# First mixer: the mix of a unit's two probabilities on GpSimd in two passes, in place of one pass on VectorE

## What is computed

```python
def diff_attend(q, k, v, lam):
    s = jnp.einsum('bqhcd,bkhcd->bhcqk', q, k, preferred_element_type=jnp.float32) * ATTN_SCALE
    p = jax.nn.softmax(s, axis=-1)
    a = p[:, :, 0] - lam * p[:, :, 1]
    return jnp.einsum('bhqk,bkhe->bqhe', a.astype(v.dtype), v)
```

## Time and profile before

| | us |
|---|---|
| Median of 3 runs | 1674.27 (1674.07 to 1675.11) |
| Profiled execution | 1675.91 |
| Its span | 1674.6 |
| TensorE busy in the span | 1648.6 (98%) |
| VectorE busy | 1127.3 (67%) |
| ScalarE busy | 825.3 (49%) |
| GpSimd busy | 240.7 (14%) |

### The profile page before, as it was taken

How to read it: one execution, slowest core, us unless ns; L and a number is a source line. 1 busy time by engine, 2 the same in 40 slices (tenths; PEclk the granted TensorE clock), 3 DMA queues, 4 the chain that set the end, 5 groups by cost and what they waited for, 6 DMA issues and landing times.

```text
span 1674.6 us, 20880 instructions
## 1 busy us (share of the span) xinstructions
PE 1648.6 (98%) x7900; PEld 1333.8 (80%) x7900; DVE 1127.3 (67%) x1320; ACT 825.3 (49%) x1022; POOL 240.7 (14%) x380
## 2 busy tenths in 40 slices
PE   6999999999999999999999999999999999999999
PEld 3776788887778888788888888888888888888887
DVE  2898778897876764766558756664666567766663
ACT  3426654435475443644446654453544447564442
POOL 0001000000002230123203002240042203002240
PEclk9999999999999999999999999999999999999999
DMA  9686188897448876677655428766676654338660
GB/s 349 221 297 220 51 303 280 312 358 256 162 126 266 265 253 201 178 225 230 213 165 168 126 76 246 219 227 183 201 214 221 213 176 151 101 124 234 210 230 26
DMA packets 250307, 346.50 MB, mean 207 GB/s; under 512 B 16160, under 2 KB 197124, under 8 KB 250208
## 3 DMA queue, kind: packets, MB, share of 16 engines
q1 hardware_dynamic: 236016, 321.95, 58.7%
q0 software_dynamic: 11488, 17.39, 4.3%
q10 hardware_dynamic: 2704, 5.82, 1.0%
HBM read 329.64 MB, written 1.05 MB: 197 GB/s over the span
## 4 chain that ended last, share of the span: by engine, by line
PE 90%; DVE 6%; ACT 2%; issue 1%; DMA 1%; SPq 0%; DVEq 0%
PE bank L467 19%; PE bank L469 19%; PE bank L468 19%; PE bank L837 7%; PE bank L838 7%; PE bank L842 7%; DVE lo L1985 1%; PE bank L1364 1%; PE bank L817 1%; PE bank L1365 1%; PE bank L1367 1%; PE bank L1175 1%; PE bank L493 1%; DMA raw<-in_ada_w 1%; PE bank L1038 1%
## 5 line engine op out<-in xcount | busy, mean ns | idle before, releaser
L1985 DVE TENSOR_TENSOR lo<-raw,hi 128x2048 fp32r<-128x2048 f32 x246 | 563.9, 2295 | 294.2 <-ACT hi L1420 290.8
L1420 ACT ACTIVATE hi<-raw 128x2048 fp32r<-128x2048 f32 x258 | 492.7, 1914 | 315.8 <-PE bank L469 172.1
L467 PE MATMUL bank<-hi,XTh 128*128 128x512 f32 (+1 forms) x1424 | 560.0, 393 | 4.8 <-DVE XTl L2096 4.5
L469 PE MATMUL bank<-hi,XTl 128*128 128x512 f32 (+1 forms) x1424 | 552.5, 388 | 0.0
L468 PE MATMUL bank<-lo,XTh 128*128 128x512 f32 (+1 forms) x1424 | 552.1, 388 | 0.0
L467 PEld LDWEIGHTS bank<-hi,XTh 128*128 128x128 f32 x1424 | 268.0, 188 | 68.5 <-issue 14.9
L469 PEld LDWEIGHTS bank<-hi,XTl 128*128 128x128 f32 x1424 | 268.0, 188 | 55.3
L468 PEld LDWEIGHTS bank<-lo,XTh 128*128 128x128 f32 x1424 | 268.3, 188 | 53.7 <-issue 1.0
L2972 POOL DMA_DIRECT2D HTR<-BLK x320 | 192.4, 609 | 735.6 <-DVE BLK L2482 688.5
L837 PE MATMUL bank<-hi,HTh 128*128 128x512 f32 x528 | 206.4, 391 | 0.0
L838 PE MATMUL bank<-lo,HTh 128*128 128x512 f32 x528 | 205.6, 389 | 0.0
(11 more groups left out here) (391 smaller groups left out, 1453.2 us busy)
## 6 DMA issues: line engine op xcount, KB each, us to landing
raw<-in_ffn_w_in SPq DMA_DIRECT2D x176, 512.0 KB, 4.9
raw<-in_ffn_w SPq DMA_DIRECT2D x132, 512.0 KB, 4.9
raw<-in_ada_w SPq DMA_DIRECT2D x96, 512.0 KB, 5.2
raw<-in_ffn_w_out SPq DMA_DIRECT2D x88, 512.0 KB, 4.1
raw<-in_w_mix_in SPq DMA_DIRECT2D x52, 512.0 KB, 4.7
raw<-in_od_pw_w SPq DMA_DIRECT2D x24, 512.0 KB, 5.5
HTR<-BLK POOLq DMA_DIRECT2D x240, 48.0 KB, 4.2
raw<-in_ev_w_in SPq DMA_DIRECT2D x20, 512.0 KB, 8.5
```

The lines of the kernel that those rows point to most:

```text
L467: pe.matmul(dst, xh, wh, start=start, stop=False)
L469: return pe.matmul(dst, xl, wh, start=False, stop=stop)
L1420: act.activation(hi[r][:, :], raw[g % RAW][:, :], ACT.Copy).then_inc(*up("hi", d))
L1985: dve.tensor_tensor(lo[r][:, :], raw[g % RAW][:, :], hi[r][:, :].bitcast(F32), ALU.subtract).then_inc(*up("lo", d))
```

## The change

The pass L2300 leaves VectorE. GpSimd gets a loop over the twelve units between its DMAs of the Fourier weights and its wait for `o_full`. For each unit it waits for the factor (`diff_rel`), multiplies P1[j] by it in place, waits for itself (`diff_scaled`), and adds P1[j] to P0[j]. The add raises `diff_mixed`, for which TensorE's transposes wait as before. VectorE's reciprocal of unit u waits for `diff_scaled` of u - 2 instead of its own `diff_rel`. The two events move to a semaphore that GpSimd raises.

```diff
--- before.py
+++ after.py
@@ -54,7 +54,7 @@
     "lambdas": "lam_prod lam_sum lam_a lam subg",
     "row_scales": "rstd_in rstd rstd2",
     "diff_scales": "diff_rstd diff_normed",
-    "diff_statistics": "diff_max diff_inv diff_rel diff_mixed",
+    "diff_statistics": "diff_max diff_inv diff_rel",
     "rotated": "rope_part roped",
     "bounds": "lb lb_diff lb_max",
     "ln_rows": "ln_sum ln_mean ln_normed ln_rstd",
@@ -68,7 +68,7 @@
     "modulations": "mods modc ada_part gate_full",
     "down_parts": "down_bias down_gated",
 
-    "hg_decays": "hg_dec hg_tail",
+    "hg_decays": "hg_dec hg_tail diff_scaled diff_mixed",
 
     "row_squares": "sq sq2 sq_in std std2",
     "exponents": "lam_exp lb_exp fox_zrow",
@@ -2289,16 +2289,13 @@
                 st = ST[:, 8 * j:8 * j + 8]
                 dve.wait_ge(*at("diff_exp", (u, 1)))
                 if u >= 2:
-                    dve.wait_ge(*at("diff_rel", u - 2))
+                    dve.wait_ge(*at("diff_scaled", u - 2))
                 dve.reciprocal(INV2[:, 2 * (u % 4):2 * (u % 4) + 2], st[:, 4:6]).then_inc(*up("diff_inv", u))
                 if u >= 2:
                     diff_values(u - 2)
                 dve.wait_ge(*at("diff_inv", u))
                 dve.tensor_scalar(st[:, 2:3], INV2[:, 2 * (u % 4) + 1:2 * (u % 4) + 2], st[:, 4:5], LAM[:, 4:5], ALU.mult,
                                   ALU.mult).then_inc(*up("diff_rel", u))
-                dve.wait_ge(*at("diff_rel", u))
-                dve.scalar_tensor_tensor(out=P0[j][:, :], in0=P1[j][:, :], scalar=st[:, 2:3], in1=P0[j][:, :], op0=ALU.mult,
-                                         op1=ALU.add).then_inc(*up("diff_mixed", u))
 
             def diff_values(u):
                 h, t = units[u]
@@ -2950,6 +2947,13 @@
             for g in range(4):
                 o = (g % 2) * HD
                 pool.dma_start(WB[o:o + HD, g // 2, o:o + HD], A["ev_fourier_w"][0, g, :, :]).then_inc(*up("four_w", g, 16))
+            for u in range(HEADS1 * T):
+                j = u % 2
+                pool.wait_ge(*at("diff_rel", u))
+                pool.tensor_scalar(P1[j][:, :], P1[j][:, :], ST[:, 8 * j + 2:8 * j + 3], None,
+                                   ALU.mult).then_inc(*up("diff_scaled", u))
+                pool.wait_ge(*at("diff_scaled", u))
+                pool.tensor_tensor(P0[j][:, :], P0[j][:, :], P1[j][:, :], ALU.add).then_inc(*up("diff_mixed", u))
             pool.wait_ge(*at("o_full", 3))
             for q in range(4):
                 pool.dma_start(TAPW[32 * q:32 * q + TAPS, :],
```

## The result

| | us |
|---|---|
| Kernel before, median of 4 runs | 1674.34 (1674.07 to 1675.11) |
| Changed kernel, median of 4 runs | 1706.45 (1704.96 to 1706.91) |
| Ratio | 1.0187 [1.0174, 1.0199] |
| Profiled execution after; its span | 1705.99; 1704.7 |

The change costs 32.1 us. The forecast was 21.1, with 1705 as the upper end: the sign was right and the size too small by a third.

A forecast was written before the change was run, and what follows sets the result against it. The prediction took a loop over VectorE and TensorE in the first mixer's stage as the bound, which GpSimd's passes lengthen. Terms 6.9 + 5.0 + 7.7 + 1.5 = 21.1 us gave 1695.4 us, range 1687 to 1705.

The forecast's parts named there:

- The loop: First mixer's stage: next mix waits for TensorE's round; 2.22 us besides the mix, turn 4.26 instead of 2.97.
- VectorE's saving: First mixer's stage: VectorE loses twelve mixes of 0.75 us, which would not count because the loop through GpSimd is longer.
- The late DMAs of the convolution's constants: DMAs at 161.08 before move behind unit 11, near 197 us; the convolution comes much later, so cost nothing.
- I take 0.8, the middle, as it reads one input: GpSimd's multiplication in each unit: 0.8 us, between a memset's 0.549 and a two-input pass's 1.036.
- the add's own term: GpSimd's add of 128x512 f32 in each unit: 1.04 us, from a tensor_tensor row of 1036 ns.
- the exclusion: Units 3 to 5: GpSimd's multiplication waits out VectorE's half split, turns of 5.3 against 3.63; 5.0 us, 3.4 less without it.
- the start: Unit 0's mixed tile comes at 148.0 us, so the work on which unit 2 hangs starts 6.9 us late.
- I take the 6.0 of w_out: Load ahead of GpSimd's first multiplication: 6.0 us, between 1.28 and 8.5.
- That cover takes the longer loop whole, 0: Turn from unit 7 to 8, 4.29 us before with VectorE waiting 1.43 for scores: the longer loop adds 0.
- The clock, 1.5 taken: Pieces behind TensorE's wait of about 8 us for unit 0 run at the lower clock: 1.5 us, ends 0 and 4.
- so this kind of work held the clock before: Argument against rival (b): transposes took 0.66 us at 140 us as at 172 in the kernel before.
- Rival (b): Clock stays low through the whole stage, up to 1.3 us a turn over nine turns: +31 to +33, 1706 us; chance 0.08.

The follow-up runs named there:

- the probe: Changed kernel plus twelve GpSimd passes of 128x512 f32 at its start, three of each form; constant 1494 ns, column 1565, two tiles 1387, broadcast column 1150; total not read.
- the fill: Changed kernel with eight discarded identity matmuls on TensorE ahead of each wait for a mixed tile from unit 2 on; 1701.18 us, ratio 1.016.
- the same edit of the start: Changed kernel with the clearing of WB and its four DMAs behind unit 1; 1706.94 us alone, 1699.55 us with eight identity matmuls ahead of each wait.

## Why the prediction was wrong in size

**The loop was right.** "Everything but the mix is 2.97 - 0.75 = 2.22 us" holds for four lengths of the mix. At full clock GpSimd's part, or VectorE's, gives:

| kernel | the mix, us | turn, us | turn - mix |
|---|---|---|---|
| before | 0.75 | 2.97 | 2.22 |
| add alone on GpSimd | 1.8 | 4.04 | 2.2 |
| broadcast multiplication | 2.42 | 4.63 | 2.2 |
| as changed | 3.0 | 5.18 | 2.2 |

VectorE's saving brought nothing, as the prediction said, and nothing behind the stage gave time back. The late DMAs of the convolution's constants (207.01) did no harm.

**"I take 0.8, the middle, as it reads one input": the term that failed first.** The multiplication took 1.56 us, above even the upper bound of 1.036, and the add 1.26 against 1.04. GpSimd's part was 3.0 us instead of 2.04. The bound was no bound: I had assumed that an instruction with one input costs no more than one with two, and the probe shows the reverse. And both the bound and the add's own term came from a row of another form, a pass with a broadcast input. In the table, freed of the clock, the dearer passes are 2.4 (units 2 to 5) + 1.8 (5 to 7) + 0.9 (7 to 8) + 2.6 (8 to 11) + 1.4 (last mix) = 9.1 us over the prediction; 0.5 of the last is the exclusion, below. With 5.9 for the clock (7.4 against 1.5) and -3.9 for the start, these are the missing 11.1.

**"I take the 6.0 of w_out" for the load: wrong, and it hid the first.** The reload cost at most the 0.12 us between the last DMA issue and the first pass, and nothing where it was moved. The Trainium skill ("GPSIMD Engine Reference", section 2.1) has about 6 us for the first call after a load; here, for this reload, the measurement decides against it. The start came out at 3.0 instead of 6.9, with the dearer passes and about 1.0 of clock in it. So the errors of the prediction partly cancelled, by luck: with the load at nothing and the rest as it stood, it would have said 15.1 us more, against the 32.1 that came.

**The exclusion was right in kind.** (The "3.4 us" that the prediction gives for it should be 3 x 1.04 = 3.1.) 2.46 against 1.56 us with a half split beside it, and 1.56 with the split moved. The rule of the Trainium skill ("SBUF — State Buffer", section "Who interferes with whom") holds here. What the prediction missed is that it also reaches the last unit, where the multiplication took 2.08 us at 203.64 with a two-input pass of VectorE, 0.69 us at 203.69, beside it. And it reaches VectorE too: its pass L2096 over 128x512 takes 0.68 or 0.69 us in the kernel before, and 1.07 where it starts inside GpSimd's add (187.20 to 188.46).

```profile
203.64 2.08 POOL L2953 TENSOR_SCALAR P<-P,ST 128x512 f32<-128x512 f32 x1 [3.54 <-DVE ST L2297]
...
203.69 0.69 DVE L2315 TENSOR_TENSOR OROW<-OROW,SS 128x512 f32<-128x512 f32 x1
...
187.94 1.07 DVE L2096 TENSOR_TENSOR XTl<-OT,XTh 128x512 fp32r<-128x512 f32 x1
```

**"That cover takes the longer loop whole, 0": right for the turn of 4.26 that it was made with, wrong for the one that came.** From unit 7 to 8 the turn was 6.06 us, 1.8 more than before. With the add alone on GpSimd, a loop of 4.04, this turn stayed at 4.28 (169.90 to 174.18), as before; a loop of 5.18 is longer than the cover, and the slower matmuls (1.06 instead of 0.61 us at 182.97 and 183.82) bring it to 6.06.

**The clock, 1.5 taken, about 8 found: the second term that failed.** For the first units, for which the 1.5 was meant, about 1.0 came. For the rest of the stage the prediction had nothing, and 7.4 came. I had argued from transposes of 0.66 us at 140 as at 172 "so this kind of work held the clock before". It did, with waits up to 0.6 us and turns of 3. The same work with waits of 2.6 in turns of 5.2 to 6.1 did not. Rival (b) named the right mechanism, and its "up to 1.3 us a turn" is the 1.27 measured, but in four turns and part of a fifth instead of nine. Rival (b) at 1706 and the result agree only because the passes were dearer as well; the prediction put the two under one head at 0.08 and did not see that the first brings the second: the longer the pass, the longer TensorE idles in each turn.

What stays open: the 7.4 us are an account from turn lengths; of them the fill showed 5.3 directly. The traces don't tell exactly when the clock falls. Before the turn at 185.56, which ran at 1.00, TensorE had worked from 176.03 to 186.68 with one wait for a mixed tile of 0.50 us, and then waited 1.84; the next wait was 2.57, and the clock fell at 193.70. But one wait of 2.61 (before 164.39) was followed by 1.00, and with the half splits moved a wait of 1.78 (before 154.06) by a low clock. The length of the last wait alone doesn't decide it.

## What to carry to other kernels

An operation with no row of its own, moved into a loop, should be priced by a probe of its very form before anything else, since every turn multiplies the error; "fewer inputs" is not a bound. Ask how long TensorE idles in each turn of the new loop: with waits of 2.0 to 2.6 us in most turns its clock fell here for parts of the stage, where with waits of at most 1.49 it did not, and then the change is paid a second time, in matmuls. A saving on an engine that only waits in that loop is worth nothing, and so is a reordering that shortens its queue alone (ratio 1.0000).

## What the runs showed of the hardware

- On GpSimd, 128x512 f32 in place: tensor_scalar 1.49 us with a constant and 1.57 with a column, tensor_tensor 1.26 to 1.28 over two tiles and 1.04 with a broadcast column, both longer in places with VectorE's work beside them. Writing a scale as a tensor_tensor with a broadcast column makes it a third cheaper. The Trainium skill ("GPSIMD Engine Reference", section 4.1) says of elementwise work there that "1-input is roughly line-rate", beside two-input operations that it calls about twice as slow as VectorE's. VectorE's tensor_scalar of this shape took 0.49 us here (with the add alone on GpSimd), a third of GpSimd's 1.56, so the measurement differs.
- VectorE's instruction with two SBUF inputs also holds off a one-input pass of GpSimd (2.46 instead of 1.56), and an add that had the whole split beside it took 3.10 us instead of 1.26 (133.79 us, with WB's DMAs behind unit 1).
- TensorE's granted clock stayed at 1.00 with waits of at most 1.49 us in turns of 4.0, and fell for parts of the stage with waits of 2.6 in turns of 5.2 to 6.1, and of 2.0 to 2.1 in turns of 4.6 to 5.5. Eight matmuls per wait on an identity held it in the turns of 5.2. Where it falls differs between executions of nearly the same program, and that hides small gains elsewhere: the same edit of the start brought about 2 us in the trace with the fill, and nothing without it.
